# A forgetting attention whose decay bias is a finished tile instead of four-row matmuls

## The chip, the core and the metric

The kernel runs on one core of a Trainium2 chip. The metric is device time in microseconds (us) for one launch; the times below are the median and the range of the runs. A core has TensorE (PE, matrix products into PSUM), VectorE (DVE), ScalarE (ACT), GpSimd (POOL) and SyncE (SP), each with an instruction stream of its own, and 16 DMA engines that all queues share. Streams wait for one another only through semaphores.

## The reference, cut to what matters

One sequence of 256 tokens of width 1024 goes through a first block of two layers and then through a second block. The diff touches the mixer of the second block:

```python
xa, ga, q, k, v, f_logit, g_a, g_b = jnp.split(h @ w_in, offs, axis=-1)
xc = causal_dwconv(xa, conv_a_w, conv_a_b)
y_a = jax.nn.gelu(ga) * rg_lru(xc, ...)
# forgetting attention, 16 heads of 64
cum = jnp.cumsum(jax.nn.log_sigmoid(f_logit + b_forget), axis=1)
sc = (q @ k.T) / 8 + cum[:, :, :, None] - cum[:, :, None, :]      # and causal mask
y_b = softmax(where(allowed, sc, -inf)) @ v
merged = sigmoid(g_a + b_merge[0]) * (y_a @ w_proj_a) + sigmoid(g_b + b_merge[1]) * (y_b @ w_proj_b)
x = x + rms_norm(merged @ w_out)
```

Everything is float32.

## The kernel before

**Slabs.** All weights pass once through a ring of five slots (`RING`), as slabs of 8 x 256 columns for each of the 128 partitions (1 MB; those of `w_proj_a` have 5 x 256, 640 KB). SyncE issues the load of a slab when the slab five before it is done on TensorE (`slab_done`). ScalarE rounds it to `w_hi` (`split_hi`, L694, three slabs ahead, `AHEAD`), VectorE makes the remainder `w_lo` (`split_lo`, L1036, two ahead), and TensorE (`gemm`, L1576) does three products a tile: high by high, high by low, low by high. That is 48 matmuls for a 1 MB slab and 30 for one of `w_proj_a`. Results go to one of two PSUM banks `ps_g`, and the engine that empties a bank counts in `emptied`.

**Order of the stages in the second block.** Each engine's stream is written out by hand in the same order: `r_xa` (5 slabs), `r_f` (the forget gate, 16 columns), `r_gate` (8), `r_ga` (5), `r_v` (4), then `r_qk` (8, queries and keys in turn), `r_pa` (`w_proj_a`, 8 short slabs, whose input is `ya_hi` and `ya_lo`), `r_pb` (4), `r_out` (4), and the feed-forward stages.

**An attention** (`attention(p, ...)`, p = 0 and 1 in the first block, p = 2 the forgetting one) handles 8 or more pairs of heads in steps. In step i TensorE does the scores of pair i (L1643, after the logits of pair i-1 have been taken out of PSUM), then a filling, then the values of pair i-3 (L1676) and the transposes of pair i-2 (L1661). VectorE makes the logits of pair i (L1076: scores plus a bias, and the row's minimum), normalises pair i-1 (L1105) and takes the low half of an output (L1136). ScalarE does the exponentials (L729) and copies. The table `FILL` says which slabs, or which chunks of the next stage, are the filling of each step. Before the attention p = 2, `IN_BEFORE[2]` = 8 slabs of `r_qk` are done; its filling of steps 0 to 7 is the 8 slabs of `r_pa`.

**The bias of the forgetting attention.** The cumulative sum `fl[:, 5, :]` (16 heads x 256 tokens, L1363) is split into a high and a low half (`fsplit`, L895 and L1366), stored to HBM (`scr_c`, L907) and loaded back by 8 small loads into `bias_q` and `bias_k` (L940, L941). These have four rows a head (two of the sum and two of ones), so that one matmul with four rows adds cum of the query less cum of the key to the scores: 4 such matmuls for each pair (L1649). The mask is a tile `causal` of 128 x 384, made on GpSimd (L646 to L649). The pair's logits need 384 columns: 128 keys for the first 128 queries, 256 for the others.

Of the kernel before, what the change touches and what calls it, by code (L numbers as in the profile page):

```python
# [12 lines left out]
P = 128  # L13
T = 256
# [43 lines left out]
    {0: [("in", 8, 0, 8)], 1: [("in", 9, 0, 8)], 2: [("in", 10, 0, 8)], 3: [("in", 11, 0, 8)], 4: [("in", 12, 0, 8)],  # L58
     5: [("in", 13, 0, 8)], 6: [("in", 14, 0, 8)], 7: [("in", 15, 0, 8)],
     8: [("out", 0, (0, 1, 2)), ("out", 1, (0, 1, 2))], 9: [("out", 0, (3, 4)), ("out", 1, (3, 4))],  # L60
     10: [("out", 0, (5,)), ("out", 1, (5,))], 11: [("out", 0, (6,)), ("out", 1, (6,))]},
# [3 lines left out]
IN_BEFORE = (5, 2, 8)  # L65
PA = 8
# [16 lines left out]
def stages():  # L83
    Stage.s = Stage.g = 0
    st = {}
    for name, n, per in (("a_in", 12, 1), ("a_out", 4, 1), ("a_up", 16, 1), ("a_dn", 16, 4),
                         ("m_in", 12, 1), ("m_out", 4, 1), ("m_up", 16, 1), ("m_dn", 16, 4),
                         ("r_xa", 5, 1), ("r_f", 1, 1), ("r_gate", 8, 1), ("r_ga", 5, 1), ("r_v", 4, 1),
                         ("r_qk", 8, 1), ("r_pa", 8, 2), ("r_pb", 4, 1), ("r_out", 4, 1),
                         ("f_up", 24, 1), ("f_dn", 12, 3)):  # L90
        st[name] = Stage(n, per)
        if name == "a_in":
            Stage.g += 5
    return st, Stage.s
# [47 lines left out]
def build(nc, ctx, t, out):  # L142
# [37 lines left out]
    rs_o = place("ffn_rs", [P, TB])  # L180
    fw = place("conv_f", [P, 4, 2 * NH2])
# [10 lines left out]
    def ar(name, shape, at, dt=F32):  # L192
# [51 lines left out]
    sga = place("sig_a", [P, NX, T], F32, nb0)  # L244
    bias_q = place("bias_q", [P, 4, T], F32R, nb0 + 8 * K)
    bias_k = place("bias_k", [P, 4, T], F32R, nb0 + 12 * K)
    causal = ar("causal", [P, 384], 68.5 * K)
    sgb = ar("sig_b", [P, NX, T], 60.5 * K)
    fl = tm("f_logsig", [16, 6, T], 0)
    fsplit = tm("f_split", [16, 2, T], 6 * K, F32R)  # L250

    prob2 = [ar("prob2_a", [P, 2, 384], 20 * K), ar("prob2_m", [P, 2, 384], 20 * K),
             ar("prob2_f", [P, 2, 384], 27 * K)]

    fqk = ar("f_qk", [P, 16, T], 0)
    fv = ar("f_v", [P, TB, D], 16 * K)
    mg = ar("merge", [P, NX, T], 51 * K)
# [53 lines left out]
    fhi, flo, fout, fin_, fones, fmask = (sem(n) for n in ("f_hi", "f_lo", "f_cum_out", "f_bias_in", "f_ones", "f_mask"))  # L311
# [9 lines left out]
    scr_c = nc.dram_tensor("cum_scr", [16, 2, T], F32, kind="Internal").ap()  # L321
# [37 lines left out]
    def att_pairs(p):  # L359
# [47 lines left out]
        else:  # L407
            qk, vv = (mqk, mv) if p == 1 else (fqk, fv)
            for i in range(8):
                units, pv = [], []  # L410
                for h, r in zip((2 * i, 2 * i + 1), halves):
                    bias = [nb[:, h, P:T], nb[:, h, :]] if p == 1 else [causal[:, 0:P], causal[:, P:384]]
                    units.append(unit(qk[r, i, :], qk[r, 8 + i, :], bias))
                    pv.append(full_pv([vv[:, tb, h * HD:(h + 1) * HD] for tb in range(TB)]))
                g = st["m_in"].g0 + 3 * (i // 2) if p == 1 else st["r_qk"].g0 + 2 * (i // 2)
                pairs.append(dict(kind="full", gate=None, out=i, start=True, stop=True, last=True, units=units, pv=pv,
                                  qk_groups=(g, g + 1), v_groups=(g + 2,) if p == 1 else ()))
# [56 lines left out]
    def _(sp):  # L474
# [92 lines left out]
        for j in range(4):  # L567
            s = st["r_v"].s0 + j
            slab(s, w_r[:, :, QKV + 2 * D + j * NS:QKV + 2 * D + (j + 1) * NS])
        for j in range(8):  # L570
            s, c0 = st["r_qk"].s0 + j, QKV + j % 2 * D + j // 2 * NS
            slab(s, w_r[:, :, c0:c0 + NS])
        groups("r_pa", rows(t["w_proj_a_2"][0]), 2, NR // 2)
# [21 lines left out]
    def _(pool):  # L595
# [45 lines left out]
        pool.wait_ge(att[1]["logit"], 2 * len(PAIRS[1]))  # L641
        pool.memset(bias_q[:, :, :].bitcast(F32), 1.0).then_inc(fones, 1)
        pool.memset(bias_k[:, :, :].bitcast(F32), -1.0).then_inc(fones, 1)
        pool.wait_ge(att[1]["pv"], len(PAIRS[1]))
        pool.wait_ge(stat_ok, 5)
        link(pool.memset(causal[:, :], 0.0))  # L646
        for c0 in (0, 2 * P):
            pool.affine_select(out=causal[:, c0:c0 + P], in_=causal[:, c0:c0 + P], compare_op=ALU.is_ge, fill=BIG, base=0,
                               pattern=[[-1, P]], channel_multiplier=1).then_inc(fmask, 1)  # L649
# [37 lines left out]
    def _(act):  # L687
# [207 lines left out]
        act.activation(fsplit[:, 0, :], fl[:, 5, :], ACT.Copy).then_inc(fhi, 1)  # L895
        for j in range(8):
# [8 lines left out]
            if j == RG_STEP:  # L905
                act.wait_ge(flo, 1)
                act.dma_start(scr_c, fsplit[:, :, :].bitcast(F32)).then_inc(fout, 16)  # L907
                act.wait_ge(sp_d, 2)
                for j in range(NR):
                    act.wait_ge(rg["ps"], j + 1)  # L910
                    act.activation(rt[:, j, :], ps_s[:, j % 2, 0:T], ACT.Sigmoid, bias=col("b_rg_a_2", j)).then_inc(act_c, 1)
                    act.activation(rix[:, j, :], ps_s[:, j % 2, T:2 * T], ACT.Sigmoid, bias=col("b_rg_x_2", j)).then_inc(rg["sig"], 1)
                    act.wait_ge(act_c, j + 1)

                    act.activation(rt[:, j, :], rt[:, j, :], ACT.Tanh, scale=sp4[:, j:j + 1]).then_inc(rg["den"], 1)
# [14 lines left out]
        for j in range(4):  # L930
            s = st["r_v"].s0 + j
            split_hi(s + AHEAD)
            tok(s, st["r_v"].g0 + j, fv[:, :, j * NS:(j + 1) * NS])
            if j == 0:
                act.wait_ge(fones, 2)
                act.wait_ge(fout, 16)
            base = 32 * j
            first = j // 2 + 2 * (j % 2)
            heads = bass.AP(tensor=scr_c.tensor, offset=first * 2 * T, ap=[[T, 2], [8 * T, 4], [1, T]])
            act.dma_start(bias_q[base + 2:base + 4, :, :].bitcast(F32), heads).then_inc(fin_, 16)  # L940
            act.dma_start(bias_k[base:base + 2, :, :].bitcast(F32), heads).then_inc(fin_, 16)  # L941
# [79 lines left out]
    def _(dve):  # L1021
# [367 lines left out]
        for j in range(8):  # L1389
            s, g = st["r_gate"].s0 + j, st["r_gate"].g0 + j  # L1390
            split_lo(s + AHEAD - 1)
            dve.wait_ge(slab_done, s + 1)
            dst = (sga if j >= 4 else sgb)[:, 2 * (j % 4):2 * (j % 4) + 2, :]
# [35 lines left out]
        def pa_slab(j, opens, closes):  # L1429
            s, g = st["r_pa"].s0 + j, st["r_pa"].g0 + j // 2  # L1430
            if opens:
                split_lo(s + AHEAD - 1)
            if closes and j % 2:
                dve.wait_ge(slab_done, s + 1)
                dve.tensor_tensor(mg[:, j - 1:j + 1, :], pair(g), sga[:, j - 1:j + 1, :], ALU.mult).then_inc(emptied[g % 2], 1)

        def qk_slab(j, opens=True, closes=True):
            if j >= PA:
                return pa_slab(j - PA, opens, closes)
# [11 lines left out]
        dve.wait_ge(fmask, 2)  # L1451
# [92 lines left out]
    def _(pe):  # L1544
# [85 lines left out]
        def attention(p, in_part, out_name, out_hi, out_lo, chunk_ready):  # L1630
# [3 lines left out]
            def scores(i):  # L1634
# [5 lines left out]
                for b in range(TB):  # L1640
                    for m, u in enumerate(pr["units"]):
                        c0, w = u["blocks"][b]
                        ins = pe.matmul(ps_s[:, m, c0:c0 + w], u["q"][:, b * P:(b + 1) * P], u["k"][b], start=True,  # L1643
                                        stop=p < 2)
                    if p == 2:
                        for m, u in enumerate(pr["units"]):
                            c0, w = u["blocks"][b]
                            r = slice(64 * m + 32 * (i % 2), 64 * m + 32 * (i % 2) + 4)
                            ins = pe.matmul(ps_s[:, m, c0:c0 + w], bias_q[r, i // 2, b * P:(b + 1) * P],  # L1649
                                            bias_k[r, i // 2, 0:w], start=False, stop=True)  # L1650
# [206 lines left out]
        for j in range(8):  # L1857
            gemm(s0 + j, g0 + j, act_hi, act_lo)
            if j == RG_STEP:
# [4 lines left out]
                for j in range(NR):  # L1864
# [8 lines left out]
                    ins.then_inc(rg["ps"], 1)  # L1873
        s0, g0 = st["r_ga"].s0, st["r_ga"].g0
# [11 lines left out]

        s0, g0 = st["r_qk"].s0, st["r_qk"].g0

        def qk_slab(j, k0=0, k1=KS):
            if j >= PA:  # L1890
                j -= PA
                gemm(st["r_pa"].s0 + j, st["r_pa"].g0 + j // 2, ya_hi, ya_lo, kc0=(j % 2) * (NR // 2), n_k=NR // 2,
                     first=j % 2 == 0, last=j % 2 == 1, before_pair=ya_in(j) if j < 2 else None)
                return
# [5 lines left out]
        pe.wait_ge(fin_, 128)  # L1900
# [57 lines left out]
```

## Time and profile before

| | |
|---|---|
| median of 3 runs | 1194.94 us (1191.47 to 1196.76) |
| the profiled execution | 1196.76 us; its span, first to last instruction, 1195.0 us |
| mean granted clock of TensorE | 0.981 of full |
| busy: TensorE, VectorE, ScalarE, GpSimd | 96%, 66%, 49%, 11% |
| stage `r_v` ends | 821.7 us |
| forgetting attention | 866.8 to 930 us |

Times in rows are microseconds from the span's start. A row of the chain of work gives start, duration and what ran; a row of a timeline also shows in brackets how long the engine was idle before it and who released it. A row of windows gives, for each engine, busy microseconds and the number of instructions in brackets, then the granted clock as a share of full, the busy share of the DMA engines, and GB/s moved.

### The profile page before, as it was taken

What the parts mean: (1) busy time and instruction counts of PE and PEld (TensorE: products, weight loads), DVE (VectorE), ACT (ScalarE), POOL (GpSimd) and SP (SyncE); (2) the same over time, 40 slices, a digit from 0 to 9 for tenths busy, and PEclk for the clock granted to TensorE, in tenths of its full rate; (3) what the DMA queues carried; (4) which work ended last, traced back from release to release, by engine and by line L of the source; (5) the groups of instructions that cost most, each with busy time, mean ns of one, the idle gap of its engine ahead of it and who ended that gap; (6) DMA issues with size and microseconds to landing.
All of it is one profiled execution on the core that took longest, in us unless ns stands there. A gap on an engine that the chain in (4) does not pass through costs nothing.

```text
span 1195.0 us, 21698 instructions
## 1 busy us (share of the span) xinstructions
PE 1144.5 (96%) x9437; PEld 1104.4 (92%) x9437; DVE 792.3 (66%) x1131; ACT 588.3 (49%) x825; POOL 130.6 (11%) x84
## 2 busy tenths in 40 slices
PE   6899899999999999999999999999999979999997
PEld 5898789999998898999999889999988879999997
DVE  5647658775436665877544888777465778888742
ACT  4257854444344555544333465655255546665531
POOL 3000040000220003100022302400000030101000
PEclk8699999999999999999999999999999989999999
DMA  9733135655554444556556471556444535556550
GB/s 274 218 106 120 58 116 178 198 180 182 197 186 142 154 134 138 177 181 197 187 177 188 114 223 36 185 169 201 136 124 142 165 117 177 181 195 207 177 177 36
DMA packets 194723, 192.67 MB, mean 161 GB/s; under 512 B 9675, under 2 KB 192692, under 8 KB 194628
## 3 DMA queue, kind: packets, MB, share of 16 engines
q1 hardware_dynamic: 191360, 188.43, 49.8%
q10 hardware_dynamic: 3268, 2.84, 1.0%
q8 instruction: 75, 1.23, 0.4%
q14 instruction: 20, 0.16, 0.0%
HBM read 189.78 MB, written 1.47 MB: 160 GB/s over the span
## 4 chain that ended last, share of the span: by engine, by line
PE 84%; DVE 8%; ACT 3%; issue 2%; ACTq 1%; POOL 1%; DVEq 0%
PE ps_gemm L1576 75%; DVE w_lo L1036 2%; PE ps_score L1643 2%; PE ps_out L1676 2%; PE ps_trans L1661 2%; PE ps_score L1871 2%; DVE xc L1347 1%; PE ps_gemm L1747 1%; ACTq L789 1%; DVE rs L1048 1%; ACTq L776 1%; DVE h_rnn L1386 0%; POOL rg_t L657 0%; PE ps_score L1649 0%; DVE act_lo L1042 0%
## 5 line engine op out<-in xcount | busy, mean ns | idle before, releaser
L1576 PE MATMUL ps_gemm<-act_hi,w_hi 128*128 128x256 f32 x1640 | 464.2, 285 | 22.8 <-ACT act_hi L970 6.7
L1576 PE MATMUL ps_gemm<-act_hi,w_lo 128*128 128x256 f32 x1640 | 459.5, 282 | 0.0
L1576 PE MATMUL ps_gemm<-act_lo,w_hi 128*128 128x256 f32 x1640 | 448.1, 282 | 0.0
L1036 DVE TENSOR_TENSOR w_lo<-raw,w_hi 128x2048 fp32r<-128x2048 f32 (+2 forms) x179 | 407.3, 2283 | 42.8 <-ACT w_hi L694 42.4
L694 ACT ACTIVATE w_hi<-raw 128x2048 fp32r<-128x2048 f32 (+2 forms) x179 | 332.5, 1862 | 175.4 <-DMA raw<-in_mlp_w 96.0
L1576 PEld LDWEIGHTS ps_gemm<-act_hi,w_hi 128*128 128x128 f32 x1640 | 312.3, 190 | 28.1 <-issue 15.7
L1576 PEld LDWEIGHTS ps_gemm<-act_hi,w_lo 128*128 128x128 f32 x1640 | 314.8, 192 | 0.2
L1576 PEld LDWEIGHTS ps_gemm<-act_lo,w_hi 128*128 128x128 f32 x1640 | 304.6, 189 | 1.5
L1576 PE MATMUL ps_gemm<-hid_hi,w_hi 128*128 128x256 f32 x512 | 143.9, 281 | 0.0
L1576 PE MATMUL ps_gemm<-hid_lo,w_hi 128*128 128x256 f32 x512 | 143.9, 281 | 0.0
L1576 PE MATMUL ps_gemm<-hid_hi,w_lo 128*128 128x256 f32 x512 | 143.9, 281 | 0.0
L1576 PEld LDWEIGHTS ps_gemm<-hid_lo,w_hi 128*128 128x128 f32 x512 | 97.2, 190 | 0.0
L1576 PEld LDWEIGHTS ps_gemm<-hid_hi,w_lo 128*128 128x128 f32 x512 | 97.2, 190 | 0.0
L1576 PEld LDWEIGHTS ps_gemm<-hid_hi,w_hi 128*128 128x128 f32 x512 | 96.1, 188 | 0.0
L839 ACT ACTIVATE hid_hi<-up_r 128x512 fp32r<-128x512 f32 x32 | 20.3, 633 | 93.1 <-DVE up_r L1259 93.1
L619 POOL TENSOR_TENSOR sq_sum<-x 128x512 f32<-128x512 f32 x5 | 12.8, 2569 | 456.3 <-DVE x L1241 225.9
L1576 PE MATMUL ps_gemm<-w_hi,act_hi 128*128 128x256 f32 (+1 forms) x192 | 57.1, 298 | 0.0
L729 ACT ACTIVATE prob<-prob,nmin 128x128 f32<-128x128 f32 (+1 forms) x92 | 39.0, 425 | 36.0 <-DVE nmin L1076 36.0
L1576 PE MATMUL ps_gemm<-w_lo,act_hi 128*128 128x256 f32 (+1 forms) x192 | 55.1, 287 | 0.0
L1576 PE MATMUL ps_gemm<-w_hi,act_lo 128*128 128x256 f32 (+1 forms) x192 | 55.1, 287 | 0.0
L1576 PE MATMUL ps_gemm<-w_hi,h_lo 128*128 128x256 f32 x192 | 53.7, 280 | 0.0
L1576 PE MATMUL ps_gemm<-w_hi,h_hi 128*128 128x256 f32 x192 | 53.7, 279 | 0.0
(305 smaller groups left out, 1691.8 us busy)
## 6 DMA issues: line engine op xcount, KB each, us to landing
raw<-in_mlp_w SPq DMA_DIRECT2D x64, 1024.0 KB, 5.2
raw<-in_w_in SPq DMA_DIRECT2D x30, 1024.0 KB, 5.4
raw<-in_w_up SPq DMA_DIRECT2D x24, 1024.0 KB, 5.2
raw<-in_od_w_in SPq DMA_DIRECT2D x12, 1024.0 KB, 5.1
raw<-in_w_down SPq DMA_DIRECT2D x12, 1024.0 KB, 5.1
raw<-in_ev_w_in SPq DMA_DIRECT2D x9, 1024.0 KB, 6.9
raw<-in_w_proj_a SPq DMA_DIRECT2D x8, 640.0 KB, 4.1
raw<-in_ev_w_out SPq DMA_DIRECT2D x4, 1024.0 KB, 5.2
```

What stands on the lines that cost most here:

```text
L619: ins = pool.tensor_tensor(dst, v, v, ALU.mult)
L694: act.activation(w_hi[:, slot, 0:k, 0:n], raw[:, slot, 0:k, 0:n], ACT.Copy).then_inc(hi_done, 1)
L729: ins = act.activation(v, v, ACT.Exp, scale=-1.0, bias=nmin[:, k, b:b + 1], accum_out=psum_[:, k, b:b + 1])
L776: act.dma_start(prow[row:row + n, tile, :], src[0:n * P].rearrange("(r c) -> r c", c=P)).then_inc(ld["par"], 16)
L789: act.dma_start(nb[a:P:8, :, :], src).then_inc(nb_in, 16)
L839: act.activation(hid_hi[:, 2 * j:2 * j + 2, :], up_r[:, j % 2, :, :], ACT.Square).then_inc(hid_h, 1)
L1036: dve.tensor_tensor(w_lo[:, slot, 0:k, 0:n], raw[:, slot, 0:k, 0:n], w_hi[:, slot, 0:k, 0:n].bitcast(F32), ALU.subtract).then_inc(w_ready, 1)
L1576: ins = pe.matmul(dst, lhs, rhs, start=(first and opens and i == 0), stop=(last and closes and i + 1 == len(order)), skip_group_check=True)
L1643: ins = pe.matmul(ps_s[:, m, c0:c0 + w], u["q"][:, b * P:(b + 1) * P], u["k"][b], start=True, stop=p < 2)
L1661: ins = pe.transpose(ps_t[0:w, 0 if pr["kind"] == "diff" else m, q * P:(q + 1) * P], prob_of(p, i)[:, m, c0:c0 + w], ident[:, :])
L1676: ins = pe.matmul(ps_o[r, pr["seq"] % 2, o0:o1], v, probs_t[0:k, m, c0:c1], start=(pr["start"] and q == 0), stop=(pr["stop"] and q == 1), ...
L1871: ins = pe.matmul(ps_s[:, j % 2, i * T:(i + 1) * T], gw[:, i, c, j - c + 1, :], xc[:, c, :], start=(q == 0), stop=(q == len(srcs) - 1))
```

## The change

The bias and the mask become one tile, `nb2` (`f_bias`, 128 partitions x 16 heads x 384), laid over the place of `ya_hi` and `ya_lo`.

- The cumulative sum is stored to HBM whole, right after it is made. When TensorE is done with `r_pa`, ScalarE issues two loads that give every partition the sums of all heads: 16 x 128 and 16 x 256 elements a partition.
- The sum of each query as a column (`fcq`, 128 x 2 x 16) comes from two transposes on TensorE after the third slab of `r_gate` and a copy on VectorE.
- GpSimd subtracts the column from the tile (over 2048 and over 4096 elements a partition) and masks two parts of it by a select over 2048 elements each. VectorE waits for this before the attention's first logits.
- The bias matmuls, `bias_q`, `bias_k`, `causal` and the split of the sum are gone.
- `r_pa` now stands between `r_v` and `r_qk`. Of `r_qk` 4 slabs are done before the attention (`IN_BEFORE`), and the other 4 are the filling of steps 0 to 3. Step 4 has none; steps 5 to 11 have one chunk of `r_pb` for each of its first two slabs (12 matmuls).
- `sig_a` moves into the room of temporary tiles, and `prob2_f` to where `sig_a` was.

```diff
-    {0: [("in", 8, 0, 8)], 1: [("in", 9, 0, 8)], 2: [("in", 10, 0, 8)], 3: [("in", 11, 0, 8)], 4: [("in", 12, 0, 8)],
-     5: [("in", 13, 0, 8)], 6: [("in", 14, 0, 8)], 7: [("in", 15, 0, 8)],
-     8: [("out", 0, (0, 1, 2)), ("out", 1, (0, 1, 2))], 9: [("out", 0, (3, 4)), ("out", 1, (3, 4))],
-     10: [("out", 0, (5,)), ("out", 1, (5,))], 11: [("out", 0, (6,)), ("out", 1, (6,))]},
+    {0: [("in", 4, 0, 8)], 1: [("in", 5, 0, 8)], 2: [("in", 6, 0, 8)], 3: [("in", 7, 0, 8)],
+     5: [("out", 0, (0,)), ("out", 1, (0,))], 6: [("out", 0, (1,)), ("out", 1, (1,))],
+     7: [("out", 0, (2,)), ("out", 1, (2,))], 8: [("out", 0, (3,)), ("out", 1, (3,))],
+     9: [("out", 0, (4,)), ("out", 1, (4,))], 10: [("out", 0, (5,)), ("out", 1, (5,))],
+     11: [("out", 0, (6,)), ("out", 1, (6,))]},
 )
-IN_BEFORE = (5, 2, 8)
-PA = 8
+IN_BEFORE = (5, 2, 4)
...
# GpSimd
+        pool.wait_ge(fin_, 32)
+        pool.wait_ge(fcq_ok, 1)
+        for c0, n, b in ((0, P, 0), (P, T, 1)):
+            link(pool.tensor_tensor(nb2[:, :, c0:c0 + n], nb2[:, :, c0:c0 + n],
+                                    fcq[:, b, :].unsqueeze(2).to_broadcast([P, 16, n]), ALU.subtract))
+            pool.affine_select(out=nb2[:, :, 2 * c0:2 * c0 + P], in_=nb2[:, :, 2 * c0:2 * c0 + P],
+                               compare_op=ALU.is_ge, fill=BIG, base=0, pattern=[[0, 16], [-1, P]],
+                               channel_multiplier=1).then_inc(fnb, 1)
...
# ScalarE
-        act.activation(fsplit[:, 0, :], fl[:, 5, :], ACT.Copy).then_inc(fhi, 1)
+        act.dma_start(scr_c, fl[:, 5, :]).then_inc(fout, 16)
...
+        for j in range(8):
+            split_hi(st["r_pa"].s0 + j + AHEAD)
+
+        act.wait_ge(fout, 16)
+        act.wait_ge(slab_done, st["r_qk"].s0)
+        for c0, n in ((0, P), (P, T)):
+            act.dma_start(nb2[:, :, c0:c0 + n], bass.AP(tensor=scr_c.tensor, offset=0, ap=[[0, P], [T, 16], [1, n]]))\
+                .then_inc(fin_, 16)
...
# VectorE
-        dve.tensor_tensor(fsplit[:, 1, :], fl[:, 5, :], fsplit[:, 0, :].bitcast(F32), ALU.subtract).then_inc(flo, 1)
+            if j == 4:
+                dve.wait_ge(fcq_ps, 1)
+                dve.tensor_copy(fcq[:, :, :], ps_s[:, 0, 0:32].rearrange("p (b h) -> p b h", b=TB)).then_inc(fcq_ok, 1)
+                dve.wait_ge(fout, 16)
...
         for j in range(IN_BEFORE[2]):
             qk_slab(j)
-        dve.wait_ge(fmask, 2)
+        dve.wait_ge(fnb, 2)
         attention(2, qk_slab)
...
# TensorE
-                    if p == 2:
-                        for m, u in enumerate(pr["units"]):
-                            c0, w = u["blocks"][b]
-                            r = slice(64 * m + 32 * (i % 2), 64 * m + 32 * (i % 2) + 4)
-                            ins = pe.matmul(ps_s[:, m, c0:c0 + w], bias_q[r, i // 2, b * P:(b + 1) * P],
-                                            bias_k[r, i // 2, 0:w], start=False, stop=True)
...
+            if j == RG_STEP + 1:
+                pe.wait_ge(fcum, 1)
+                pe.wait_ge(rg["sig"], NR)
+                for tb in range(TB):
+                    ins = pe.transpose(ps_s[:, 0, tb * 16:(tb + 1) * 16], fl[:, 5, tb * P:(tb + 1) * P], ident[0:16, 0:16])
+                ins.then_inc(fcq_ps, 1)
...
+        for j in range(8):
+            gemm(s0 + j, g0 + j // 2, ya_hi, ya_lo, kc0=(j % 2) * (NR // 2), n_k=NR // 2,
+                 first=j % 2 == 0, last=j % 2 == 1, before_pair=ya_in(j) if j < 2 else None)
...
-        pe.wait_ge(fin_, 128)
+        pe.wait_ge(fcq_ok, 1)
```

## Rows read from the trace of the kernel before

**Rows 1.** The page: engine totals, and the chain that ended last.

```profile
PE 1144.5 (96%) x9437; PEld 1104.4 (92%) x9437; DVE 792.3 (66%) x1131; ACT 588.3 (49%) x825; POOL 130.6 (11%) x84
...
PE 84%; DVE 8%; ACT 3%; issue 2%; ACTq 1%; POOL 1%; DVEq 0%
```

**Rows 2.** Windows: the stretch from the end of `r_v` to the attention's end.

```profile
821.70:866.80 45.10, 45.10 (x386) 44.97 (x384) 20.15 (x15) 15.39 (x11) 0.00 (x0) 1.00 0.50 153
866.80:930.00 63.20, 63.20 (x522) 53.34 (x521) 37.01 (x108) 35.35 (x87) 0.00 (x0) 1.00 0.39 126
```

**Rows 3.** The chain in order of time, q/k slabs and one attention step.

```profile
799.98 66.87 PE ps_gemm L1576 x575
...
872.10 0.42 PE ps_score L1643 x4
...
872.78 0.63 PE ps_score L1643 x4
...
873.72 3.62 PE ps_gemm L1576 x30
```

**Rows 4.** The chain in order of time, one step of the second attention.

```profile
423.97 0.80 PE ps_out L1676 x8
424.77 0.81 PE ps_trans L1661 x6
425.58 0.86 PE ps_score L1643 x8
```

**Rows 5.** The chain in order of time, after the forget gate.

```profile
709.46 0.43 ACT f_split L895
...
710.39 2.20 DVE w_lo L1036
...
717.80 18.37 PE ps_score L1871 x84
```

**Rows 6.** Timeline of ScalarE and its queue, two moments.

```profile
17.37 0.63 ACTq L789 DMA_DIRECT2D bias<-bias_wide_scr  x1
...
821.67 0.48 ACT L716 ACTIVATE f_v<-ps_gemm,rs_tok 128x256 f32<-128x256 f32 x1 [2.80 <-PE ps_gemm L1576]
```

**Rows 7.** Windows: the rate of the DMA engines in three stretches.

```profile
1090.00:1091.00 1.00, 1.00 0.60 184
...
1091.00:1095.00 4.00, 4.00 (x37) 4.00 (x36) 3.42 (x7) 2.43 (x2) 0.00 (x0) 1.00 0.98 353
...
17.40:41.50 24.10, 20.07 (x140) 19.59 (x139) 18.86 (x35) 6.39 (x6) 1.08 (x2) 0.81 1.11 258
```

**Rows 8.** Timeline of SyncE's queue, the load of `gain_row`.

```profile
1089.46 0.58 SPq L581 DMA_DIRECT2D gain_row<-in_ffn_norm_post  x1
```

**Rows 9.** Instructions that touch `bias`: durations in ns, first and last start.

```profile
L631 POOL TENSOR_SCALAR_AFFINE_SELECT bias<-bias x1: 2005/2005/2005, 41.5 to 41.5; 128x2048 f32<-128x2048 f32 x1
```

**Rows 10.** Groups of instructions on GpSimd: busy us and mean ns, idle before.

```profile
L652 POOL TENSOR_TENSOR rg_ix<-rg_ix,xc 128x256 f32<-128x256 f32 x10 | 7.3, 730 | 57.5 <-ACT rg_ix L912 57.5
L656 POOL TENSOR_TENSOR rg_t<-rg_t,rg_r 128x1280 f32<-128x1280 f32 x2 | 5.9, 2966 | 19.0 <-ACT rg_t L920 19.0
```

**Rows 11.** Timeline of GpSimd, one operation beside VectorE.

```profile
759.89 4.90 POOL L657 TENSOR_TENSOR rg_t<-rg_t,rg_ix 128x1280 f32<-128x1280 f32 x1
```

**Rows 12.** Timeline of VectorE, first and last instruction of one pair's logits.

```profile
868.63 0.29 DVE L1076 CUSTOM_DVE_ANT_0 prob<-ps_score,causal 128x128 f32<-128x128 f32 x1 [1.05 <-PE ps_score L1649]
...
869.75 0.08 DVE L1076 DVE_READ_ACCUMULATOR2_ANT nmin<- 128x1 f32 x1
```

**Rows 13.** Windows: TensorE's clock after a wait, near the start.

```profile
30.00:35.00 5.00, 1.16 (x8) 0.88 (x8) 4.91 (x9) 1.09 (x1) 0.00 (x0) 0.83 1.08 283
35.00:40.00 5.00, 4.81 (x22) 4.84 (x23) 4.78 (x17) 0.00 (x0) 0.00 (x0) 0.50 1.15 230
```

**Rows 14.** Timeline of VectorE, logits of two steps of the first attention.

```profile
128.36 0.29 DVE L1076 CUSTOM_DVE_ANT_0 prob<-ps_score,bias 128x128 f32<-128x128 f32 x1 [1.48 <-PE ps_score L1643]
...
132.78 0.29 DVE L1076 CUSTOM_DVE_ANT_0 prob_a<-ps_score,bias 128x128 f32<-128x128 f32 x1 [2.42 <-PE ps_score L1643]
```

More of the change, by code:

```diff
@@ L88, in stages @@
                          ("r_xa", 5, 1), ("r_f", 1, 1), ("r_gate", 8, 1), ("r_ga", 5, 1), ("r_v", 4, 1),
-                         ("r_qk", 8, 1), ("r_pa", 8, 2), ("r_pb", 4, 1), ("r_out", 4, 1),
+                         ("r_pa", 8, 2), ("r_qk", 8, 1), ("r_pb", 4, 1), ("r_out", 4, 1),
                          ("f_up", 24, 1), ("f_dn", 12, 3)):
@@ L180, in build @@
     rs_o = place("ffn_rs", [P, TB])
+    fcq = place("f_cum_q", [P, TB, 16])
     fw = place("conv_f", [P, 4, 2 * NH2])
@@ L243, in build @@
     gt = ar("gelu_tmp", [P, 2, 2, T], 0)
[L244 to L247, printed above, removed]
+    sga = tm("sig_a", [P, NX, T], 0)
     sgb = ar("sig_b", [P, NX, T], 60.5 * K)
     fl = tm("f_logsig", [16, 6, T], 0)
-    fsplit = tm("f_split", [16, 2, T], 6 * K, F32R)
     prob2 = [ar("prob2_a", [P, 2, 384], 20 * K), ar("prob2_m", [P, 2, 384], 20 * K),
-             ar("prob2_f", [P, 2, 384], 27 * K)]
+             place("prob2_f", [P, 2, 384], F32, nb0)]
     fqk = ar("f_qk", [P, 16, T], 0)
     fv = ar("f_v", [P, TB, D], 16 * K)
+    nb2 = ar("f_bias", [P, 16, 384], 27 * K)
     mg = ar("merge", [P, NX, T], 51 * K)
@@ L310, in build @@
     fz, fa, fcum = sem("f_z"), sem("f_act"), sem("f_cum")
-    fhi, flo, fout, fin_, fones, fmask = (sem(n) for n in ("f_hi", "f_lo", "f_cum_out", "f_bias_in", "f_ones", "f_mask"))
+    fout, fin_, fcq_ps, fcq_ok, fnb = (sem(n) for n in ("f_cum_out", "f_bias_in", "f_cq_ps", "f_cq_ok", "f_nb"))
     pbm, pbh, pbl = sem("pb_m"), sem("pb_hi"), sem("pb_lo")
@@ L320, in build @@
     scr_w = nc.dram_tensor("bias_wide_scr", [16, 16 * REL], F32, kind="Internal").ap()
-    scr_c = nc.dram_tensor("cum_scr", [16, 2, T], F32, kind="Internal").ap()
+    scr_c = nc.dram_tensor("cum_scr", [16, T], F32, kind="Internal").ap()
     def col(name, i=0, n=1):
@@ L411, in att_pairs @@
                 for h, r in zip((2 * i, 2 * i + 1), halves):
-                    bias = [nb[:, h, P:T], nb[:, h, :]] if p == 1 else [causal[:, 0:P], causal[:, P:384]]
+                    bias = [nb[:, h, P:T], nb[:, h, :]] if p == 1 else [nb2[:, h, 0:P], nb2[:, h, P:384]]
                     units.append(unit(qk[r, i, :], qk[r, 8 + i, :], bias))
@@ L569, in _ @@
             slab(s, w_r[:, :, QKV + 2 * D + j * NS:QKV + 2 * D + (j + 1) * NS])
+        groups("r_pa", rows(t["w_proj_a_2"][0]), 2, NR // 2)
         for j in range(8):
@@ L572, in _ @@
             slab(s, w_r[:, :, c0:c0 + NS])
-        groups("r_pa", rows(t["w_proj_a_2"][0]), 2, NR // 2)
         for name, w in (("r_pb", "w_proj_b_2"), ("r_out", "w_out_2")):
@@ L640, in _ @@
         ins.then_inc(gz, 1)
[L641 to L649, printed above, removed]
         for j in range(NR):
@@ L905, in _ @@
             if j == RG_STEP:
-                act.wait_ge(flo, 1)
-                act.dma_start(scr_c, fsplit[:, :, :].bitcast(F32)).then_inc(fout, 16)
                 act.wait_ge(sp_d, 2)
@@ L933, in _ @@
             tok(s, st["r_v"].g0 + j, fv[:, :, j * NS:(j + 1) * NS])
[L934 to L941, printed above, removed]
+        for j in range(8):
[5 more added lines that the diff above has]
+                .then_inc(fin_, 16)
         def qk_slab(j, opens=True, closes=True):
@@ L1363, in _ @@
         dve.tensor_tensor_scan(fl[:, 5, :], fl[:, 0, :], fl[:, 2, :], 0.0, ALU.mult, ALU.add).then_inc(fcum, 1)
-        dve.wait_ge(fcum, 1)
-        dve.wait_ge(fhi, 1)
-        dve.tensor_tensor(fsplit[:, 1, :], fl[:, 5, :], fsplit[:, 0, :].bitcast(F32), ALU.subtract).then_inc(flo, 1)
         def decay(j):
@@ L1428, in _ @@
         dve.wait_ge(gs2, 8)
-        def pa_slab(j, opens, closes):
+        for j in range(8):
             s, g = st["r_pa"].s0 + j, st["r_pa"].g0 + j // 2
-            if opens:
-                split_lo(s + AHEAD - 1)
-            if closes and j % 2:
+            split_lo(s + AHEAD - 1)
+            if j % 2:
                 dve.wait_ge(slab_done, s + 1)
@@ L1437, in qk_slab @@
         def qk_slab(j, opens=True, closes=True):
-            if j >= PA:
-                return pa_slab(j - PA, opens, closes)
             s, g = st["r_qk"].s0 + j, st["r_qk"].g0 + j
@@ L1642, in scores @@
                         c0, w = u["blocks"][b]
-                        ins = pe.matmul(ps_s[:, m, c0:c0 + w], u["q"][:, b * P:(b + 1) * P], u["k"][b], start=True,
-                                        stop=p < 2)
-                    if p == 2:
-                        for m, u in enumerate(pr["units"]):
-                            c0, w = u["blocks"][b]
-                            r = slice(64 * m + 32 * (i % 2), 64 * m + 32 * (i % 2) + 4)
-                            ins = pe.matmul(ps_s[:, m, c0:c0 + w], bias_q[r, i // 2, b * P:(b + 1) * P],
-                                            bias_k[r, i // 2, 0:w], start=False, stop=True)
+                        ins = pe.matmul(ps_s[:, m, c0:c0 + w], u["q"][:, b * P:(b + 1) * P], u["k"][b], start=True, stop=True)
                 ins.then_inc(a["score"], 1)
@@ L1885, in ya_in @@
             return wait
+        for j in range(8):
+            gemm(s0 + j, g0 + j // 2, ya_hi, ya_lo, kc0=(j % 2) * (NR // 2), n_k=NR // 2,
+                 first=j % 2 == 0, last=j % 2 == 1, before_pair=ya_in(j) if j < 2 else None)
         s0, g0 = st["r_qk"].s0, st["r_qk"].g0
         def qk_slab(j, k0=0, k1=KS):
[L1890 to L1894, printed above, removed]
             s, g = st["r_qk"].s0 + j, st["r_qk"].g0 + j
```

## The prediction

> **What bounds the kernel now.** I read the engine totals and the chain of work first [rows 1]: TensorE (PE) is busy 96% of the span and holds 84% of the chain that ended last. So a change counts by what it does to TensorE's stream, and any gap opened in that stream is paid in full. Then the stretch that the diff touches, as windows [rows 2]: from 821.7 to 930.0 us TensorE is busy without a gap at full granted clock (1.00, that is 2.4 GHz), while VectorE is at about half and GpSimd (POOL) does nothing at all. Then the chain in that stretch [rows 3], which gives the prices: 575 projection matmuls in 66.87 us is 0.1163 us each, so a slab of 48 takes 5.58 us and a short slab of `w_proj_a` (30 matmuls) 3.49 us. One early step of the forgetting attention starts at 872.10: scores and bias matmuls 1.62 us, then from 873.72 a short slab of 3.62. No wait of TensorE is in it. The short slabs are what TensorE does while VectorE and ScalarE work off the logits.
>
> **The change, part by part.**
>
> *Bias matmuls gone.* The scores with their bias take 1.62 us a step [rows 3]; eight score matmuls alone took 0.86 us in the second attention [rows 4]. The difference, 0.76 us, is paid in 8 steps: -6.1 us, all on TensorE's path.
>
> *The low half of the cumulative sum gone.* The ScalarE copy and the VectorE subtraction stand in the chain one after the other from 709.46 to 710.39, with TensorE waiting behind them for its recurrence matmuls at 717.80 [rows 5]: -0.9 us. Two small transposes are added after the third gate slab. They wait for the last sigmoid of the recurrence, which ends before that slab of 5.58 us does. They, and the 32-column copy on VectorE, are given 0.3 us together. So -0.6 us. The memsets and selects taken off GpSimd come off an engine that is busy 11% of the span [rows 1]: nothing.
>
> *`w_proj_a` moved ahead of q/k.* The same matmuls in another order. `r_v` ends at 821.6 (ScalarE empties its last group at 821.67 [rows 6]). Eight short slabs follow, to 821.6 + 8 x 3.49 = 849.5. `ya_lo` is finished in the stage before `r_v`, four slabs (22 us) earlier, so nothing is missing. The raw loads keep up: during the short slabs a 1 MB load has to land every 3.49 us, and one moves at 353 GB/s when the engines are full [rows 7], 3.0 us. Four q/k slabs then end at 849.5 + 4 x 5.58 = 871.8.
>
> *The new tile.* `nb2` lies over `ya_hi` and `ya_lo`, so its load can start only when TensorE has finished `w_proj_a`, at 849.5. ScalarE waits for that with its queue behind it (the high halves of q/k slabs 3 and on). Slab 3 is wanted at 866.3, so this wait has some 12 us of cover.
>
> The load is 128 x 16 x 384 x 4 bytes = 3.15 MB. How fast? Upper rate: the one load whose source is also one row for all partitions, `gain_row`, was issued at 1089.46 [rows 8] behind a slab load, and the two moved at 353 GB/s from 1091 to 1095, after half a rate in the slice from 1090 [rows 7]. Alone at that rate `nb2` takes 8.9 us, and with 1.1 us to the first bytes it lands at 859.5. Lower rate: the eight loads of the first bias tile (2.1 MB, issued from 17.37, in place at 41.5, when the select on them starts) took 24.1 us while the engines moved 258 GB/s [rows 6, 7, 9], so they had a third of the traffic, 86 GB/s; that gives 36.6 us and 887.2. Here one slab load (1.05 MB per 5.58 us) is in flight beside it, not a queue of them, so I take half of a rate between the two (305 / 2 = 153 GB/s): 20.6 us, landed at 849.5 + 1.1 + 20.6 = 871.2.
>
> The Trainium skill, page "DMA: Bandwidth & Descriptors", section "Queues, rings and completion order", says that each DMA engine goes round-robin between the queue rows that have work, a packet at a time. By that rule the load gets about the half that I took, and the sum below stands; the row of the first bias tile does not agree with it (a third), and by that row the sum would be 16 us more.
>
> *GpSimd's work on it.* Two subtractions (2048 and 4096 elements per partition) and two selects. Its tensor operations grow from 0.730 us at 256 elements to 2.966 at 1280 [rows 10], 2.18 ns an element and 0.17 fixed: 4.6 + 9.1 us. A select over 2048 took 2.0 us [rows 9]: 4.0 for two. With the joins 18.0 us. Beside busy VectorE one operation over 1280 elements took 4.90 us, 3.8 ns an element [rows 11], which would make it 27.5; but VectorE soon has nothing to do here. So the tile is ready at 871.2 + 18.0 = 889.2, between 877.3 and 914.7.
>
> *The stall.* VectorE waits for the tile before the first logits. Behind that wait stand the logits, the emptying of q/k slab 4 and all later low halves. TensorE passes its own new wait at once: it does score 0 (0.86) and slab 4 (5.58), to 871.8 + 0.86 + 5.58 = 878.3, and then needs the logits of pair 0 for score 1. Those take 1.2 us (868.63 to 869.83, start of the last plus its 0.08 [rows 12]) after the tile: 890.5. Stall 12.2 us; from the ends of load and GpSimd, 0.3 to 37.7.
>
> *Clock.* After a stretch in which TensorE was busy 1.16 of 5 us, the next 5 us ran at 0.50 (1.2 GHz) [rows 13]. Five us at half clock cost 2.5 us (0 to 5).
>
> *The attention's filling.* Steps 0 to 3 carry 48-matmul slabs, step 4 none, steps 5 to 7 only 12 matmuls (1.42 us). Without filling a step is values 0.80, transposes 0.81 and scores 0.86 [rows 4], 2.5 us of TensorE, and 3.9 with 12 matmuls. In the first attention two logits without a slab between stood 4.42 us apart [rows 14]; if that were the floor, steps 4 to 7 lose 1.9 + 3 x 0.5 = 3.4 us. But that attention has more VectorE work per pair; TensorE can do values and transposes while logits are made. I take +1.0. Total matmuls of slabs and output parts are otherwise unchanged, and from the last `act_lo` on both kernels run the same.
>
> **Sum.** -6.1 - 0.6 + 12.2 + 2.5 + 1.0 = +9.0 us. Against the profiled execution's 1196.8 that is 1205.8. That execution is the slowest of the three, 1.8 above the median of 1194.9, so the median of the new kernel comes to 1204.
>
> **Rivals.**
> (A) The tile is in time. If the load has the DMA engines nearly to itself (landed at 859.5) and GpSimd keeps 18 us, the tile is there at 877.5, and score 1 is hardly late. Then only the gain is left: -6.7 + 0.5 + 0.5 = -5.7, or 1189. It decides at a landing before some 860. For it: 353 GB/s of [rows 7]. Against: the q/k slabs are streaming then, taking 188 GB/s by themselves. 12 in 100.
> (B) The load goes at the pace of the first bias tile: landed 887.2, ready 905.2, stall 28.2: -6.7 + 28.2 + 2.5 + 1.0 = +25.0, or 1220; with contended GpSimd 9 more, 1229. For it: the only load of this shape in the trace, rows of at most 1 KB on ScalarE's queue. Against: that was the crowded start. 18 in 100.
> (C) As forecast, but the thin steps 4 to 7 are bound by the chain of logits and exponentials: 2.5 us more, 1206.5. 8 in 100.
>
> **How the numbers follow.** The forecast (stall 5 to 21 us, 1197 to 1213) has 62 in 100, and the likeliest is 1204. The range 1190 to 1222 reaches from A to B's middle and leaves out the best of A and the contended half of B, under 2 in 10. A difference of 0.5% (6 us, 1189.0 to 1200.9) is about what can be told from none. Faster than that is half of A and a little of the rest: 0.08. Within: the other half of A and stalls below some 9 us: 0.22. Slower: 0.70.
>
> **What would show it.** In the profile after: the `f_bias` loads issued near 849 and landed near 871; GpSimd busy some 18 us on `f_bias`; VectorE idle until it; one TensorE wait of about 12 us between q/k slab 4 and score 1 with half clock behind it; score steps of 0.86 us without `bias_q`. The prediction fails if the load lands before 862 or after 885, or if a wait at slab 3 (late high half) comes ahead of it.

## The result: 0.8% slower

The changed kernel takes 1201.93 us in the median of 5 runs (1201.20 to 1205.07) against 1194.94: a ratio of 1.0083, 95% interval 1.0061 to 1.0104. On another chip, beside three of the experiments, it was 1.0095 (1.0060 to 1.0129). Forecast were 1204 and +9.0 us; measured are +7.0, and +10.0 on that other chip.

The profiled execution took 1203.53 us, its span is 1201.7. Engine totals and the chain's shares, from the page:

```profile
PE 1142.1 (95%) x9407; PEld 1103.9 (92%) x9407; DVE 792.0 (66%) x1131; ACT 587.8 (49%) x824; POOL 144.6 (12%) x83
...
PE 81%; DVE 6%; ACT 4%; DMA 3%; POOL 2%; ACTq 1%; issue 1%; SPq 1%; DVEq 0%; POOLq 0%
```

Beside [rows 1], TensorE gave up three points of the chain, and DMA, which had no share, now has 3%: a load has come onto the path. The chain in order of time shows which one (start, duration, what):

```profile
851.86 0.42 ACTq L936
852.31 20.49 DMA f_bias<-cum_scr
...
872.87 4.79 POOL f_bias L651
...
877.80 2.00 POOL f_bias L653
879.81 7.00 POOL f_bias L651
...
886.94 2.02 POOL f_bias L653
...
888.98 0.29 DVE prob L1072
...
890.33 1.65 PE ps_score L1637 x8
```

The list of waits puts a number on it (microseconds in total, times, longest), and the windows show the clock behind it (columns as in [rows 2]):

```profile
PE ps_score L1637 <- DVE nmin L1072: 10.1, 1, 10.1
```

```profile
860.00:870.00 10.00, 10.00 (x91) 10.00 (x90) 4.36 (x4) 1.62 (x2) 0.00 (x0) 1.00 1.10 344
...
880.00:885.00 5.00, 0.23 (x2) 0.03 (x1) 0.00 (x0) 0.00 (x0) 5.00 (x1) 0.84 0.63 210
885.00:890.00 5.00, 0.00 (x0) 0.00 (x0) 1.02 (x7) 0.34 (x2) 3.80 (x2) 0.50 0.00 0
890.00:895.00 5.00, 4.67 (x28) 4.05 (x29) 4.96 (x15) 4.75 (x16) 0.00 (x0) 0.63 0.00 0
```

TensorE's queue stands still for 10.1 us between q/k slab 4 and score 1. In that time, up to the logits at 888.98, GpSimd is the only engine at work. While TensorE was idle the granted clock fell to 0.50 (1.2 GHz), and it came back to full between 890 and 900; the first scores after it took 1.65 us instead of 0.86.

**A ruler for the experiments.** Whole times of one kernel differ by several us, and most of this arises before the change: the first high half of the second block starts at 656.2 us in the trace of the kernel before and at 658.7 in that of the changed one, with the same code up to there, and in the 14 traces of this study anywhere from 644.7 to 661.9. So I also read the stretch from the last `f_v` to the last output of the attention, by the last starts on ScalarE:

```profile
L714 ACT ACTIVATE f_v<-ps_gemm,rs_tok x8: 454/468/475, 811.6 to 825.0; 128x256 f32<-128x256 f32 x8
L738 ACT ACTIVATE act_hi<-ps_out x8: 360/383/384, 913.4 to 937.5; 128x256 fp32r<-128x256 f32 x8
```

These are of the changed kernel: 825.0 and 937.5, so 112.5 us. The same two rows of the kernel before end at 822.0 and 930.0, 108.0 us:

```profile
L716 ACT ACTIVATE f_v<-ps_gemm,rs_tok x8: 452/468/477, 808.2 to 822.0; 128x256 f32<-128x256 f32 x8
L740 ACT ACTIVATE act_hi<-ps_out x8: 383/383/385, 889.4 to 930.0; 128x256 fp32r<-128x256 f32 x8
```

So the stretch holds +4.5 of the +6.7 us between the spans. The rest: +2.5 up to the second block, +0.5 from there to `f_v`, -0.8 behind the attention. All three lie within what one kernel differs by. From the second block to `f_v` the kernel before takes 165.8 us in its own trace and 167.2 and 167.8 in those of experiments 3 and 4, whose code is the same up to there.

**The ruler has a scatter of its own.** The changed kernel's second trace has 115.1 us for this stretch, 2.6 more, though its wait is shorter (9.5 us). The reason stands in the starts of the projection matmuls: they follow one another every 0.113 us or every 0.118, in blocks of tens of microseconds. Both spacings come at a granted clock of 1.00. TensorE in 20 us of short slabs in each of the two traces (columns: busy us, matmuls in brackets, granted clock, DMA share, GB/s), first the changed kernel, then the same kernel again:

```profile
826.00:846.00 20.00, 20.00 (x179) 1.00 0.72 230
```

```profile
827.00:847.00 20.00, 20.00 (x172) 1.00 0.70 216
```

What sets the spacing no run here shows. Each wide spacing costs 0.0045 us. In the stretch the kernel before has 462 of them, the changed kernel 198, and its second trace 652. Taking off 0.0045 us for each gives the last column of the table below. There the two traces of each kernel that was traced twice agree within 0.7 us, and the change costs 5.8 or 6.3 us where the raw stretch says 4.5 or 7.1. The spacing also makes most of the scatter ahead: the trace that reaches the second block first, at 644.7 us, has 898 wide spacings up to there against 3826 in the kernel before, which is 13.2 us, and it is 11.5 earlier.

### The profile page after: what moved, and what is told of

Same layout as the page of the kernel before. It is cut to its first block, busy times and chain, and to the rows that moved or that the text cites. A ratio compares the mean times of both kernels' runs of the same rounds, so it can differ in the third digit from the quotient of the medians.

```text
span 1201.7 us, 21631 instructions
## 1 busy us (share of the span) xinstructions
PE 1142.1 (95%) x9407; PEld 1103.9 (92%) x9407; DVE 792.0 (66%) x1131; ACT 587.8 (49%) x824; POOL 144.6 (12%) x83
## 4 chain that ended last, share of the span: by engine, by line
PE 81%; DVE 6%; ACT 4%; DMA 3%; POOL 2%; ACTq 1%; issue 1%; SPq 1%; DVEq 0%; POOLq 0%
PE ps_gemm L1570 72%; PE ps_score L1637 2%; DVE w_lo L1032 2%; PE ps_out L1663 2%; DMA f_bias<-cum_scr 2%; PE ps_trans L1648 2%; PE ps_score L1858 2%; SPq L547 1%; POOL f_bias L651 1%; DMA raw<-in_w_in 1%; ACTq L787 1%; ACT w_hi L692 1%; PE ps_gemm L1734 1%; ACTq L774 1%; DVE h_rnn L1379 1%
## 5 line engine op out<-in xcount | busy, mean ns | idle before, releaser
L1570 PE MATMUL ps_gemm<-w_lo,h_hi 128*128 128x256 f32 x192 | 53.1, 276 | 0.0
```

What stands on the lines that cost most here:

```text
L1570: ins = pe.matmul(dst, lhs, rhs, start=(first and opens and i == 0), stop=(last and closes and i + 1 == len(order)), skip_group_check=True)
```

## The experiments

The ratio is to the kernel before on the same chip. The stretch is from the one profile of each; the last column is the stretch as it would be with every projection matmul at the narrow spacing.

| run | ratio (95%) | median us | stretch us | at the narrow spacing |
|---|---|---|---|---|
| kernel before | 1 | 1194.9 | 108.0 | 105.9 |
| changed kernel | 1.0083 (1.0061 to 1.0104) | 1201.9 | 112.5 | 111.7 |
| changed kernel again | 1.0095 (1.0060 to 1.0129) | 1205.0 | 115.1 | 112.2 |
| bias matmuls left out of before | 0.9974 (0.9937 to 1.0011) | 1188.5 | 102.2 | 99.8 |
| order alone | 1.0012 (0.9978 to 1.0045) | 1194.4 | 106.1 | 105.7 |
| tile in four pieces | 0.9995 (0.9967 to 1.0022) | 1191.8 | 101.9 | 100.6 |
| the same again | 0.9981 (0.9955 to 1.0007) | 1192.3 | 101.5 | 100.2 |
| no subtraction | 0.9995 (0.9966 to 1.0024) | 1192.0 | 103.0 | 100.0 |
| two more GpSimd operations | 1.0155 (1.0120 to 1.0190) | 1216.1 | 127.6 | 126.6 |
| the same again | 1.0200 (1.0165 to 1.0234) | 1219.5 | 128.8 | 125.9 |
| loads on SyncE's queue | 1.0016 (0.9996 to 1.0037) | 1199.5 | 110.4 | 107.5 |
| SyncE's queue, no subtraction | 0.9965 (0.9940 to 0.9990) | 1193.2 | 103.0 | 100.0 |
| and the last q/k slab split | 0.9957 (0.9937 to 0.9977) | 1191.4 | 102.7 | 99.7 |
| the same again | 0.9977 (0.9949 to 1.0004) | 1191.5 | 100.8 | 99.7 |

Experiments 1 to 4 ran on one chip, 5, 6 and the first two runs of 7 on a second, and the four repeats on a third. The median of the kernel before was 1192.6, 1197.7 and 1195.0 us on these three; on the first its runs ranged from 1183.0 to 1203.7.

**1. The tile in four pieces.**

```diff
-        for c0, n in ((0, P), (P, T)):
-            act.dma_start(nb2[:, :, c0:c0 + n], ...).then_inc(fin_, 16)
+        for q in range(4):                      # heads 4q to 4q+3
+            for c0, n in ((0, P), (P, T)):
+                act.dma_start(nb2[:, 4 * q:4 * q + 4, c0:c0 + n], ...).then_inc(fin_[q], 16)
 # (cut) GpSimd: subtraction and select per piece, after fin_[q] only
 # VectorE: wait for the pair's own piece before its logits
```

> The changed kernel with the tile in four pieces of four heads: each piece has its own two loads, GpSimd works piece by piece, and VectorE waits only for the piece of the pair at hand. Same bytes, same GpSimd elements, same order of stages. Theory L (the whole loss is TensorE's one wait of 10.1 us for the finished tile and 1.7 us of slow clock behind it): the first piece (0.79 MB) lands some 6 us after its issue and is ready 4 us later, long before score 1; wait gone, 1202 - 12 = 1190 us, 0.4% faster than the kernel before. Rival O (the moved stage and the thin steps 4 to 7 cost the time, and the wait only uses time that would be lost there anyway): it stays at 1198 or above. Rival T (3.15 MB more traffic delays the slabs' own loads): the traffic is the same, so it stays near 1202.

Stretch 101.9, 10.6 less than the changed kernel's (11.1 at equal spacing); TensorE's wait is gone and 10 us of time with it, with the same bytes, the same elements and the same order. That excludes theories O and T. The ratio, 0.9995 and 0.9981, is above the 0.996 expected, and both intervals hold 1.

**2. No subtraction.**

```diff
-        pool.wait_ge(fcq_ok, 1)
         for c0, n, b in ((0, P, 0), (P, T, 1)):
-            link(pool.tensor_tensor(nb2[...], nb2[...], fcq[:, b, :] ..., ALU.subtract))
             pool.affine_select(...)
```

> The changed kernel without the subtraction of the query's own sum: that term is the same for all keys of a query and cancels in the softmax, so the result is the reference's. GpSimd keeps the two selects (4.0 us) of its 16.1; the two transposes and the copy of the column go too. One load as before. Theory L: tile ready at about 877, 3 us before score 1 wants its logits; wait at most 1 us; 1202 - 12 - 0.5 = 1189.5 us. Rival O: 1198 or above. If the GpSimd term were not on the path (the load alone sets it): 1202.

The load was as slow as before (GpSimd's first select starts at 873.35), but with 4.9 us of GpSimd instead of 16.1 the tile is ready at 878.2 and TensorE does not wait. So the GpSimd work is on the path, and removing it suffices; the two transposes and the small copy that went with it cost some 0.2 us.

**3. The bias matmuls alone.** The four matmuls for each pair at L1649 taken out of the kernel before.

> The kernel before with the 32 bias matmuls left out (so the forgetting attention lacks its decay) and all else kept. By the step periods of the chain 0.76 us a step: 1195 - 6.1 = 1189 us. By the bias records' own time, 0.58 us a step: 1190.4. If the attention's steps are bound elsewhere, 1195.

Stretch -5.8 us, and -6.1 at equal spacing. The period of the steps is the right price (6.1), the records' own time (4.6) is too low. The medians lie 4.1 us apart, and the interval of the ratio (-7.5 to +1.3 us) cannot tell that from either price, nor from nothing.

**4. The order alone.** `r_pa` ahead of `r_qk` on all five engines, `IN_BEFORE[2]` and `FILL[2]` as in the change, everything else as before.

> The kernel before with the order alone changed: w_proj_a ahead of q/k, four q/k slabs before the attention, four in steps 0 to 3, thin steps from 4 on. Bias matmuls and the small loads stay. Theory L: the order costs about 1 us, 1195 + 1 = 1196. Rival O: 4 us or more, 1199 and up.

Stretch 106.1: 1.9 us shorter than before, not 1 longer. But 1.7 us of that is the spacing of the matmuls (76 wide ones against 462), and at equal spacing 0.2 are left. The time, 1.0012 (0.9978 to 1.0045), cannot be told from zero, but it excludes a loss of 6 us or more. That the order costs nothing fits its parts. Eight short slabs between two attention steps took 3.62 us each [rows 3], while in a row they took 27.2 us (824.6 to 851.8 in the changed kernel), 3.4 each: some 1.8 gained. Four 48-matmul slabs now stand between the steps, at 5.65 to 5.85 us instead of 5.44 in a row at the narrow spacing, and the output's chunks come in smaller portions: most of it lost again. In this trace TensorE does not wait in the thin steps at all.

**5. Twice the suspected cost.**

```diff
-            link(pool.tensor_tensor(nb2[...], nb2[...], fcq..., ALU.subtract))
+            for op in (ALU.subtract,) if b == 0 else (ALU.subtract, ALU.add, ALU.subtract):
+                link(pool.tensor_tensor(nb2[...], nb2[...], fcq..., op))
```

> The changed kernel with GpSimd's subtraction over 4096 elements followed by an addition and a subtraction of the same column: two more operations of 7.0 us each, nothing else changed. Theory L (TensorE's wait for the tile is paid in full): tile 14.1 us later, wait 10.1 + 14.1 = 24 us, 1202 + 14 = 1216 us, 1.020 of the kernel before. If part of the wait were slack that something later gives back: less than 10 more.

The trace says 14.2 us more of waiting, for 14.1 us more of GpSimd:

```profile
PE ps_score L1638 <- DVE nmin L1073: 24.3, 1, 24.3
```

The stretch grew by 15.1 us. The ratio was only 0.7% above that of the changed kernel from another chip, so both were run again on one:

> The changed kernel itself once more, on one chip with the next three, since the kernel before moved by 5 us between two calls. 1.008 of the kernel before.

> The run with two more GpSimd operations once more. In its trace the stretch from the end of the values' projection to the attention's end was 15.1 us longer than the changed kernel's (127.6 against 112.5), yet its ratio was only 0.7% above the changed kernel's, from another call. If the wait is paid in full: 15 us (1.3%) above the changed kernel on the same chip, 1.020 of the kernel before.

On one chip: 1219.5 against 1205.0 us, +14.5, for 14.0 us more of waiting (23.5 against 9.5). The wait is paid in full, one for one. On the other chip the kernel before was 2.7 us slower and this one 3.5 us faster, which together gave the low ratio; why is not shown.

**6. The loads on SyncE's queue.**

```diff
         for j in range(8):                      # SyncE, r_qk
+            if j == 4:
+                sp.wait_ge(fout, 16)
+                sp.wait_ge(slab_done, st["r_qk"].s0)
+                for b0, n in ((0, P), (P, T)):
+                    sp.dma_start(nb2[:, :, b0:b0 + n], ...).then_inc(fin_, 16)
             slab(s, w_r[:, :, c0:c0 + NS])
```

> The changed kernel with its two loads issued on SyncE's queue, between the loads of q/k slabs 3 and 4, instead of on ScalarE's. Theory S (the 20.5 us to landing come from sharing the DMA engines with the slab loads): now nothing else is in flight, so 3.15 MB at some 345 GB/s land 9 to 11 us after 850, at 860 to 861; with 16 us of GpSimd and 1.2 of logits the tile is just in time at 878 to 880, wait 0 to 1 us, 1190 to 1191 us. Slab 4's load follows at 861, is ready at 869 and wanted at 873: no wait. Rival (the form of this load, 512 B and 1 KB rows that all partitions read from one place, is slow by itself): it lands near 870 again, wait near 8 us, 1200.

It landed 13.2 us after its issue instead of 20.5, at 864.6, so the form of the load is not slow, and sharing explains the 20.5. It is still later than the 860 to 861 expected, for the next slab loads were issued from 853.4 on and the engines moved 276 to 351 GB/s for both. And the wait fell only to 4.6 us, because the earlier tile brought GpSimd's work beside VectorE's: its last two operations took 3.9 us longer than by themselves. By an estimate from these rows, 0.7 us of wait would be left without that. Timeline of GpSimd in this run:

```profile
864.64 3.61 POOL L657 TENSOR_TENSOR f_bias<-f_bias,f_cum_q 128x2048 f32<-128x2048 f32 x1 [92.78 <-DMA f_bias<-cum_scr]
868.40 2.00 POOL L659 TENSOR_SCALAR_AFFINE_SELECT f_bias<-f_bias 128x2048 f32<-128x2048 f32 x1
870.38 9.06 POOL L657 TENSOR_TENSOR f_bias<-f_bias,f_cum_q 128x4096 f32<-128x4096 f32 x1
879.59 3.87 POOL L659 TENSOR_SCALAR_AFFINE_SELECT f_bias<-f_bias 128x2048 f32<-128x2048 f32 x1
```

and of VectorE at the same time:

```profile
869.56 2.99 DVE L1032 TENSOR_TENSOR w_lo<-raw,w_hi 128x2048 fp32r<-128x2048 f32 x1 [6.63 <-ACT w_hi L698]
...
873.08 8.51 DVE L1032 TENSOR_TENSOR w_lo<-raw,w_hi 128x2048 fp32r<-128x2048 f32 x1
```

The subtraction over 4096 elements took 9.06 us instead of 7.02: it stood behind the first low half, which ended at 872.55. The second low half, which takes 2.28 us alone, took 8.51: it started under the subtraction, and ended 2.15 us after it. In those 2.15 us the last select stood (3.87 instead of 2.00). So each waited for the other's whole instruction, and the expected 0 to 1 us of waiting was wrong by a reason that the prediction had priced only from GpSimd's side. Behind the wait the next slab took 7.82 us instead of 5.86, the slow clock again. The Trainium skill, page "GPSIMD Engine Reference", section "1. Specifications", has GpSimd and VectorE share their SBUF interfaces, with contention when VectorE has two SBUF inputs; these rows agree.

**7. Toward a version that beats both.** First both remedies:

> Both remedies: loads on SyncE's queue and no subtraction (the query's own sum cancels in the softmax). Tile ready near 866, 14 us before it is wanted, and ScalarE's queue is not held by the issue. Theory L: nothing is left but the gain of the bias matmuls and the thin steps' loss of 1.3 us: 1189 to 1190, the same as the kernel with the tile in pieces and the one without the subtraction.

The tile was ready at 869.9 and no wait for it was left; stretch 103.0, time 0.9965 (0.9940 to 0.9990). Then the filling:

```diff
-    {0: [("in", 4, 0, 8)], ..., 3: [("in", 7, 0, 8)],
+    {0: [("in", 4, 0, 8)], ..., 3: [("in", 7, 0, 4)], 4: [("in", 7, 4, 8)],
```

> As the run with both remedies, and the last q/k slab split over steps 3 and 4 of the attention, so that step 4 has a filling. If step 4's 1.3 us of waiting come from its missing filling, 1.3 us less: 1188. If they come from the chain of logits, exponentials and normalising that follows from steps 4 on, no change.

The pieces of the chain between 872 and 923 are now all TensorE's, so the wait behind step 4 is gone. But that wait was 0.3 us in the run with both remedies, not the 1.3 expected (see the thin steps below), and the stretch became 0.3 shorter (102.7 for 103.0, both with the wide spacing throughout). The time (0.9957 for 0.9965) moved by less than it can tell. Pieces and this version once more:

> The run with the tile in four pieces once more. Stretch 101.9 us in its trace, 10.6 less than the changed kernel's: 0.9% below it, 0.9995 of the kernel before as measured, or 0.995 as the stretch has it (6.1 less than before's 108.0).

> The run with loads on SyncE's queue, no subtraction and the last q/k slab split, once more: stretch 102.7, 5.3 less than before's: 0.9957 of the kernel before.

0.9957 and 0.9977: by these two, 0.2 to 0.4% or some 3 to 5 us faster than before; the first interval leaves out 1, the second (to 1.0004) just holds it. It is 1% faster than the change.

## Why the prediction was right, step by step

- **Bias matmuls, -6.1 us.** Right: -5.8 in the stretch when they alone are left out, -6.1 at equal spacing.
- **Low half of the sum, -0.6.** Mis-sized: some -0.1. From the start of the scan to the recurrence's first matmul the kernel before and experiments 3 and 4 take 9.05 us, and all traces with the change 8.68 to 8.70: 0.36 less instead of 0.9. The two transposes cost some 0.24: the three gate slabs with them took 17.2 us, which is 144 matmuls at the wide spacing (16.96) and 0.24. The chain suggests why the first fell short:

```profile
711.57 0.69 DVE f_logsig L1359
712.28 0.32 ACTq L893
...
712.66 1.92 ACT w_hi L692
...
714.60 1.28 ACT L901
715.89 0.91 ACT sig_b L901 x2
```

  The store now stands in ScalarE's queue waiting for the scan, with a high half, a table load and the sigmoids queued behind it. I had counted what VectorE no longer does, but not what ScalarE's new wait holds back. In the way up to `f_v` (165.8 to 167.8 us without the change, 166.3 in both traces with it) so little cannot be seen.
- **The load, landed 21.7 us after `w_proj_a` ends.** Right: 21.0 (851.8 to 872.8). It went at 154 GB/s (3.15 MB in 20.5 us), somewhat under half of the 344 that the engines moved, with the slabs' loads on the other queue. The Trainium skill, page "DMA: Bandwidth & Descriptors", section "Queues, rings and completion order", has each DMA engine go round-robin between the queues that have work; this trace is near the half that I took by it, not the third of [rows 7]. Experiment 6 shows that this sharing is the reason.
- **GpSimd, 18.0 us.** 16.1: the operation over 4096 elements took 7.02, not 9.1, and that over 2048 took 4.79, of which 1.31 us lie under a low half of VectorE (871.89 to 874.18). Without one it took 3.61 (experiment 6). That is 1.7 ns an element at either length. My 2.18 came from products of two full tiles [rows 10], and here one input is a column; whether that is the reason was not tried.
- **The stall, 12.2 us.** 10.1: those two terms make 2.6 us less, and TensorE came to the wait 0.4 earlier than forecast. Experiments 1, 2 and 5 show it as cause: with the tile in pieces, or without GpSimd's subtraction, it goes, and with 14.1 us more, 14.5 come out. The load on the other queue took 5.5 of it away.
- **Clock, +2.5.** Between 1.4 and 2.6: scores 0.8 longer, and slab 5 longer than the next by 0.6 in the first trace (6.45 for 5.85) and by 1.8 in the second (7.68 for 5.86), where the granted clock was still 0.66 from 895 to 900.
- **Thin steps, +1.0.** With the order at most 0.3. TensorE waits once in them, 0.30 us. Timeline of TensorE:

```profile
915.01 0.87 PE L1663 MATMUL ps_out<-prob_t_f,f_v 128*64 128x256 f32 x8
915.82 0.88 PE L1648 MATMUL ps_trans<-ident,prob_f 128*128 128x128 f32 x6
916.62 0.93 PE L1637 MATMUL ps_score<-f_qk 64*128 64x128 f32 x8
917.85 0.35 PE L1570 MATMUL ps_gemm<-act_hi,w_hi 128*128 128x256 f32 x1 [0.30 <-DVE act_lo L1132]
```

  Between 914.99 and 917.85 it does the values, transposes and scores of step 5, and then needs the low half of output 0 for its first chunk. The expectations of experiment 7 took 1.3 us for this wait; that left out the scores. The floor of 4.42 us a step from the first attention did not hold: steps 5 to 7 went by in 4.07. The order as a whole, which I had at zero, gave 0.2 us in its own trace at equal spacing.

The sum: forecast -6.7 + 12.2 + 2.5 + 1.0 = +9.0. Measured in the stretch, at equal spacing: -6.1 + 10.1 + 1.4 + 0.3 - 0.2 = +5.5, for 5.8 between the two profiles, and -6.1 + 9.5 + 2.6 + 0.3 - 0.2 = +6.1, for 6.3 in the second trace (the low half's -0.1 lies ahead of the stretch). So the mechanism and its parts are right, and the stall was sized 2 us too long. That the whole time moved by 7.0 and 10.0 us, nearer to 9.0 than the stretch did, is then scatter outside the stretch, and luck. What stays open: at equal spacing the versions without the wait are 5.3 to 6.2 us shorter than before in the stretch, but 0.6 to 5 us in time. The spacing of the matmuls can move a whole run by more than that, and which spacing the timed runs had is not recorded.

## What to carry to other kernels

Small matmuls that add a rank-two bias on the fly look wasteful, but they need no tile: replacing them by a finished tile puts a broadcast load and a GpSimd pass in series, and when the tile's room comes free only just before its first use, that series is the path. Cut such a tile along the order in which it is used, and drop from it whatever the following operation cancels, before asking whether the engine that makes it is fast. Price a load by its share beside the other queue's traffic, and a GpSimd pass by what VectorE does at that moment, in both directions.

## What the runs showed of the hardware

GpSimd and VectorE can hold each other for the whole length of an operation, here a low half of VectorE, which reads two tiles in SBUF. In the run with the tile in pieces the same subtraction of 512 elements took 1.04 or 3.07 us, and the same select 0.64 or 2.49:

```profile
859.49 1.04 POOL L655 TENSOR_TENSOR f_bias<-f_bias,f_cum_q 128x512 f32<-128x512 f32 x1 [86.69 <-DMA f_bias<-cum_scr]
860.68 0.64 POOL L657 TENSOR_SCALAR_AFFINE_SELECT f_bias<-f_bias 128x512 f32<-128x512 f32 x1
...
863.93 3.07 POOL L655 TENSOR_TENSOR f_bias<-f_bias,f_cum_q 128x512 f32<-128x512 f32 x1
867.15 2.49 POOL L657 TENSOR_SCALAR_AFFINE_SELECT f_bias<-f_bias 128x512 f32<-128x512 f32 x1
```

The long ones lie under VectorE's low halves (863.77 for 2.33 us, 866.63 for 2.52). In these rows whichever started second waits for the rest of the first (8.51 us for 2.28 on VectorE's side, above). The logits, which read PSUM and one tile in SBUF, took their usual 0.28 and 0.41 us beside a subtraction of 1.03.

Projection matmuls of one form followed one another every 0.113 or every 0.118 us at the same granted clock of 1.00, in blocks, in one and the same kernel. Up to the second block alone it made 13.2 us between two traces, more than the 7.0 of the change, so two traces should be compared at equal spacing.

Eight loads issued in a row on ScalarE's queue kept that queue for 11.5 us (850.2 to 861.8), with the high halves behind them, where two larger ones kept it for 4.6.
